# Moving the small tensors below the large ones in on-chip memory, so that the weight buffers and the activations all start at multiples of 1024 bytes

## The reference

```python
h = rms_norm(x, norm_mix)
proj = h @ w_in                      # 2048 x 5656, split into three head groups
out_a = ...                          # gated linear attention, 4 heads
out_b = ...                          # mLSTM matrix memory, 4 heads
out_c = ...                          # spatial gating, 4 groups
x = x + concat(out_a, out_b, out_c) @ w_out      # 2048 x 2048
hf = rms_norm(x, norm_ffn)
gate, up = split(hf @ w_gu)          # 2048 x 11264
x = x + (silu(gate) * up) @ w_down   # 5632 x 2048
return rms_norm(x, norm_final)
```

## The kernel before

| tensor | size | start before | remainder | start after | remainder |
|---|---|---|---|---|---|
| ident | 512 | 114816 | 128 | 16512 | 128 |
| cols, stat, stat_b | 144, 384, 320 | 115328 and on | | 17024 and on | |
| raw | 16384 | 16512 | 128 | 18432 | 0 |
| w_hi | 16384 | 32896 | 128 | 34816 | 0 |
| w_lo | 16384 | 49280 | 128 | 51200 | 0 |
| hT_hi | 16384 | 65664 | 128 | 67584 | 0 |
| hT_lo | 16384 | 82048 | 128 | 83968 | 0 |
| x1 | 16384 | 98432 | 128 | 100352 | 0 |
| mixT_hi, actT_hi | 16384, 45056 | 116736 | 0 | 116736 | 0 |
| mixT_lo | 16384 | 133120 | 0 | 133120 | 0 |
| actT_lo | 45056 | 161792 | 0 | 161792 | 0 |
| act_tok | 4096 | 210944 | 0 | 210944 | 0 |

## Time and profile before

### The profile page before, as it was taken

The page is one execution under the profiler, slowest core; times in us unless marked ns, Lnnn a source line. Parts: engine busy times, 40 slices in busy tenths (PEclk is TensorE's granted clock), DMA queues, the critical chain, the costliest instruction groups (busy, mean ns, idle before and its releaser), DMA issues.

```text
span 1134.3 us, 13836 instructions
## 1 busy us (share of the span) xinstructions
PE 1121.3 (99%) x5211; PEld 932.8 (82%) x5211; DVE 628.6 (55%) x709; ACT 512.7 (45%) x608; POOL 41.5 (4%) x66
## 2 busy tenths in 40 slices
PE   8999999999999999999999999999999999999996
PEld 7898889888888888888888888888888888888885
DVE  5456767698565555554555555555555545454443
ACT  6445535555445544444443444444434434343432
POOL 2700000000010000000000000000000000000000
PEclk9999999999999999999999999999999999999999
DMA  8665646554475676666666666666666555556552
GB/s 277 207 204 154 191 126 193 160 166 150 151 252 176 183 224 194 191 188 188 185 187 199 185 185 190 188 195 185 186 195 189 183 190 187 186 187 191 192 189 94
DMA packets 110058, 211.09 MB, mean 186 GB/s; under 512 B 6844, under 2 KB 11008, under 8 KB 109632
## 3 DMA queue, kind: packets, MB, share of 16 engines
q1 hardware_dynamic: 108960, 205.75, 59.6%
q0 software_dynamic: 1056, 4.77, 1.2%
HBM read 208.40 MB, written 2.10 MB: 186 GB/s over the span
## 4 chain that ended last, share of the span: by engine, by line
PE 98%; DMA 1%; ACT 0%; SPq 0%; DVE 0%; issue 0%; ACTq 0%; POOLq 0%; POOL 0%
PE acc L984 31%; PE acc L986 31%; PE acc L985 31%; PE mx L976 2%; PE mx L1155 1%; PE mx L1061 1%; DMA tok<-in_x 1%; ACT x L544 0%; PE mx L1139 0%; PE mx L1046 0%; PE mx L1183 0%; PE mx L1210 0%; PE acc L1002 0%; PE acc L1003 0%; SPq L207 0%; PE acc L1006 0%
## 5 line engine op out<-in xcount | busy, mean ns | idle before, releaser
L563 DVE TENSOR_TENSOR w_lo<-raw,w_hi 128x1024 fp32r<-128x1024 f32 (+2 forms) x392 | 470.4, 1204 | 470.3 <-ACT w_hi L332 469.8
L332 ACT ACTIVATE w_hi<-raw 128x1024 fp32r<-128x1024 f32 (+2 forms) x392 | 408.2, 1044 | 546.6 <-PE acc L986 537.1
L984 PE MATMUL acc<-w_hi,hT_hi 128*128 128x512 f32 (+2 forms) x1084 | 419.0, 387 | 0.0
L986 PE MATMUL acc<-w_hi,hT_lo 128*128 128x512 f32 (+2 forms) x1084 | 415.9, 384 | 0.0
L985 PE MATMUL acc<-w_lo,hT_hi 128*128 128x512 f32 (+2 forms) x1084 | 415.8, 384 | 0.0
L986 PEld LDWEIGHTS acc<-w_hi,hT_lo 128*128 128x128 f32 x1084 | 203.6, 188 | 40.1
L984 PEld LDWEIGHTS acc<-w_hi,hT_hi 128*128 128x128 f32 x1084 | 203.7, 188 | 39.2 <-ACT tok L357 0.4
L985 PEld LDWEIGHTS acc<-w_lo,hT_hi 128*128 128x128 f32 x1084 | 203.7, 188 | 38.8
L984 PE MATMUL acc<-w_hi,actT_hi 128*128 128x512 f32 x352 | 139.1, 395 | 0.0
L985 PE MATMUL acc<-w_lo,actT_hi 128*128 128x512 f32 x352 | 139.0, 395 | 0.0
L986 PE MATMUL acc<-w_hi,actT_lo 128*128 128x512 f32 x352 | 139.0, 395 | 0.0
(11 more groups left out here) (192 smaller groups left out, 471.9 us busy)
## 6 DMA issues: line engine op xcount, KB each, us to landing
raw<-in_w_gu SPq DMA_DIRECT2D x176, 512.0 KB, 3.7
raw<-in_w_down SPq DMA_DIRECT2D x88, 512.0 KB, 3.6
raw<-in_w_in SPq DMA_DIRECT2D x80, 512.0 KB, 4.2
raw<-in_w_out SPq DMA_DIRECT2D x32, 512.0 KB, 4.2
raw<-in_w_in SPq DMA_DIRECT2D x8, 272.0 KB, 2.9
raw<-in_w_in SPq DMA_DIRECT2D x8, 264.0 KB, 2.8
tok<-in_x SPq DMA_DIRECT2D x8, 256.0 KB, 7.5
x<-in_x POOLq DMA_DIRECT2D x2, 1024.0 KB, 8.6
```

Of the source, the lines that this page charges most:

```text
L332: act.activation(w_hi[:, slot, 0:UC * width], raw[:, slot, 0:UC * width], ACT.Copy)\
L563: dve.tensor_tensor(w_lo[:, slot, 0:UC * width], raw[:, slot, 0:UC * width], w_hi[:, slot, 0:UC * width].bitcast(F32), ALU.subtract).then_ ...
L984: pe.matmul(o, hi[:, c + i, tb], wh, start=first and i == 0, stop=False)
L986: ins = pe.matmul(o, lo[:, c + i, tb], wh, start=False, stop=last and i == UC - 1)
```

## The change

The six large tensors `raw`, `w_hi`, `w_lo`, `hT_hi`, `hT_lo` and `x1` are allocated after the four small ones instead of before them, and `raw` with `align=1024`. All six sizes are multiples of 1024, so all six start at multiples of 1024. `ident`, `cols`, `stat` and `stat_b` go to the bottom. What is allocated later keeps its addresses. No instruction is added, removed or moved on any engine's queue; only addresses in the instructions differ.

```diff
-        raw = sb("raw", [P, R, UC * GW])
-        w_hi = sb("w_hi", [P, R, UC * GW], F32R)
-        w_lo = sb("w_lo", [P, R, UC * GW], F32R)
-        hT_hi = sb("hT_hi", [P, KC, T], F32R)
-        hT_lo = sb("hT_lo", [P, KC, T], F32R)
-        x1 = sb("x1", [P, NB, D])
         ident = sb("ident", [P, P])
         cols = sb("cols", [P, 36])
         stat = sb("stat", [P, 96])
...
-
+        raw = sb("raw", [P, R, UC * GW], align=1024)
+        w_hi = sb("w_hi", [P, R, UC * GW], F32R)
+        w_lo = sb("w_lo", [P, R, UC * GW], F32R)
+        hT_hi = sb("hT_hi", [P, KC, T], F32R)
+        hT_lo = sb("hT_lo", [P, KC, T], F32R)
+        x1 = sb("x1", [P, NB, D])
         early = ExitStack()
         mixT_hi = sb("mixT_hi", [P, KC, T], F32R, early, align=1024)
         mixT_lo = sb("mixT_lo", [P, KC, T], F32R, early, align=1024)
```

## The result

The changed kernel takes 1128.6 us (median of 4 runs, 1128.33 to 1129.21) against 1136.0 us, a ratio of 0.993 with a 95% interval of 0.9919 to 0.9942. The forecast was 1127.8 us.

The account below looks back on a forecast made before the run. The prediction took TensorE's wide matmuls to bound the kernel. The 1440 with `mixT` and `actT` would gain 8.2 us, all other terms 0, so 1136.0 - 8.2 = 1127.8 us, with a range of 1125 to 1138 us.

Parts of the forecast that it names:

- the rival without an effect: Height in memory, not remainder, makes `mixT` and `actT` slow, so nothing moves: 1136.0 us, chance 0.24.
- Only TensorE's cost per matmul can move the time: Whole kernel: TensorE busy 1121.3 of 1134.3 us, waiting only at the start; time is its instruction count times their cost.
- The 5.7 ns: Extra cost of each 512-column matmul with a `mixT` or `actT` tile (232.5 ns) over one with `hT` (226.7 ns).
- Likeness of the two starts: Moving columns and stationary tile starting at the same remainder by 1024 give 226.7 ns instead of 232.5 ns.
- the slow case: Rival: a tile at remainder 0 is what costs, so `hT` matmuls slow too, 17.4 us, 1153.4 us; chance 0.14.
- a collision of the loaded tile with the moving columns: Reason for choosing likeness: TensorE's two streams, moving columns and next stationary tile, collide depending on their distance.
- the untried pair 0 and 0: Columns and tile both at remainder 0, absent from the earlier trace; bounded by 226.7 and 232.5 ns, taken as 226.7.
- 1440 matmuls by 5.7 ns, 8.2 us: Gain claimed for the wide matmuls with `mixT` (384) and `actT` (1056) tiles: 8.2 us.
- `raw`, `x1` and the small tensors: 0: Their new addresses cost or gain 0 us: `raw` accesses are covered, the others touch TensorE only in transposes.
- No effect, for height: Rival: the higher part of memory, where `mixT` and `actT` stay, costs the 5.7 ns; 1136.0 us, chance 0.24.
- Its second support: Narrow matmuls, second row block at 192 against tiles at 128: 11.5 ns excess against 13.4 in wide ones, so distance seemed free.
- A larger gain: Rival: half the 13.4 ns excess in all 4500 wide matmuls goes, 30 us more, about 1098 us; chance 0.05.

Follow-up runs that it names:

- e9: TensorE alone, nothing of the layer computed: rows of 60 matmuls, each row with its own operand starts; 226.7 ns per matmul at distance 256, 232.3 at 128.
- e1: Changed kernel with everything that the matmuls read starting 128 bytes past a multiple of 1024: 1128.56 us, ratio 0.9929 to the kernel before.
- e2: Changed kernel with `w_hi` and `w_lo` 128 bytes lower (and `raw` 512 lower to make room): 1153.27 us, ratio 1.0145 to the kernel before.
- e4: Changed kernel with `hT` (and `x1`) 32, `mixT` 64 and `actT` 256 bytes past a multiple of 1024: 1149.36 us in one execution.
- e5: Changed kernel with `mixT_lo` and `actT_lo` alone starting 128 bytes past a multiple of 1024: 1133.82 us in one execution.
- e6: Changed kernel with hi tensors at multiples of 256 and lo tensors, `w_lo` too, 128 bytes past one: 1146.79 us, ratio 1.0088 to the kernel before.
- e3: Changed kernel with `raw` alone moved, to start at remainder 640: 1128.08 us, ratio 0.9924 to the kernel before.
- e10: TensorE alone, rows of 30 matmuls of 512 columns, tile 0, 4, 8 ... 252 bytes past a multiple of 1024, columns at one: none below 226.7 ns.

## Why the prediction was right

The range of 1125 to 1138 us also holds 1136.0, the time of the rival without an effect. The time near 1127.8 us and the pitches in the two stages are what tells them apart.

1. *Only TensorE's cost per matmul can move the time.* Shown: no wait appeared or went, and 8.1 us went from the two stages where the pitch fell. The whole span closes with it: 7.3 us shorter, 8.1 us less in these stages and 1.0 us more at the start, with 0.2 us less elsewhere.
2. *The 5.7 ns come from where the operands lie, not from other engines, DMAs or the clock.* Shown by e9, with nothing beside TensorE and a granted clock of 1.00.
3. *Likeness of the two starts decides.* Shown between the rivals that I had. e1 excludes the slow case, in which a tile at remainder 0 is what costs, and e2 shows that such a tile is slow or fast with the place of the weights. Agreement by 256 bytes is enough: e4 and e9 have 226.7 ns with the tile 256 bytes off, and e9 has 232.3 at 128. The trace of before already said that 1024 is not it: with `hT` the tiles of the second token block started at 640, but the moving columns stayed at 128; the prediction has both at 640, which is a wrong reading. The reason given for it, a collision of the loaded tile with the moving columns, is not shown: the rows of e5, e6 and e9 with alternating starts contradict each simple form of it. So taking 226.7 ns for the untried pair 0 and 0 was a choice between two values, for a reason that no run bears out; that choice was part luck.
4. *1440 matmuls by 5.7 ns, 8.2 us.* Measured 8.1 us in the stages. Of the 1.4 us by which the profiled execution, at 1129.2 us, missed the forecast, 1.0 us lies ahead of L983, 0.8 of it at the lower clock, and 0.5 us lies outside the span: the time is 2.2 us longer than the span here, and was 1.7 us longer before; the rest of the span gives 0.1 us back. The executions at the higher mean clock missed it by 0.5 and 0.6 us.
5. *`raw`, `x1` and the small tensors: 0.* Shown for `raw` by e3. `x1` and the small ones were not moved by themselves; the stages and the start leave 0.2 us of the span for them and for everything else.
6. *No effect, for height.* Excluded: `actT` has kept its place and lost its 5.7 ns. Its second support, that a distance of 64 bytes costs nothing in the narrow groups, was a wrong reading. The tiles lay 64 bytes below the columns of the second row block there, a distance of 192, which costs 2.2 ns at 512 columns (64 above costs 6.6). And the excess over the columns' own time can't be compared between widths: with equal starts it is 13.4 ns at 512 columns, and at 256 it goes from 6.6 to 13.4 ns with the distance.
7. *A larger gain.* Excluded for these starts: the pitch with both at 0 is the one with both at 128, and e10 found no distance with less. The Trainium skill has 518 cycles for 512 columns ("TensorE: Matmul & The Clock Gate", "Back-to-back issue gap"), 215.8 ns, as the gap of an isolated matmul. No run here comes near it: fp32r matmuls of that width with a load each never settled below 226.7. The skill also states that TensorE's two read ports are independent and that TensorE never waits on anyone ("SBUF — State Buffer", "Who interferes with whom"). No run here can show the ports, but it doesn't follow that the place of the operands is free: their starts alone are worth 0 to 11 ns per matmul.

## What to carry to other kernels

Where TensorE is the bound, read the pitch of the same matmul in each stage. Here two pitches at one clock, with no wait, were a question of where the operands lie, and the stretch where the DMAs and the other engines rest was the place to ask it. For fp32r matmuls of 512 columns, start the stationary tiles and the moving columns at the same remainder by 256 bytes; an absolute multiple of 1024 is not needed, and in this layer moving the weights alone cost 2% (e2, 1153.3 against 1128.6 us). For other widths measure first, since at 256 columns a distance of 64 was 6.9 ns better than none.

## What the runs showed that was not expected

- With equal starts the pitch is steady, 226 or 227 ns each time (544 cycles at 2.4 GHz). With most other distances it runs in a repeating pattern: at 128 in e9, every seventh or eighth distance is 240 or 241 ns and the others are 228 to 233.
- From 384 to 512 columns with equal starts the pitch goes from 173.3 to 226.7 ns, 0.417 ns per column, which is one cycle at 2.4 GHz. The excess over that time of the columns is 13.4 ns at 512 columns and 13.3 at 384, but 6.6 ns at 256 columns with a distance of 64.
- Equal distances don't always give equal pitches (252: 226.7 and 236.6 ns), and even the same two starts, 0 and 128, had 232.3 ns in e9 and 233.5 in e10. What else it depends on is open.
